# A two-layer decoder trunk on one core: memory values formed with tokens on the partitions, value halves side by side, and the step orders rewritten

## What is computed

```python
def memory_branch(q_mem, mem, norm_mem, w_mem_kv):
    k_m, v_m = jnp.split(rmsnorm(mem, norm_mem) @ w_mem_kv, 2, axis=-1)
    q, k, v = _heads(q_mem, 4), _heads(k_m, 4), _heads(v_m, 4)
    sc = jnp.einsum('bqhd,bkhd->bhqk', q, k) * 64 ** -0.5
    p = jax.nn.softmax(sc, axis=-1)
    return jnp.einsum('bhqk,bkhd->bqhd', p, v).reshape(q_mem.shape)
```

## Time and profile before

| what | us |
|---|---|
| median of 3 runs | 1217.27 (1217.08 to 1217.52) |
| the profiled execution | 1217.43 |
| its span, first to last instruction | 1215.6 |
| granted clock, mean | 0.999 of full speed |
| first memory tile begins | 14.9 |
| memory steps of layer A | 60 to 98 |
| attention of layer A and output projection | 98 to 285 |
| feed-forward part A | to 640 |
| memory steps of layer B | 655 to 694 |
| attention of layer B and output projection | 694 to 850 |

### The profile page before, as it was taken

The page is one execution under the profiler, slowest core; times in us unless marked ns, Lnnn a source line. Parts: engine busy times, 40 slices in busy tenths (PEclk is TensorE's granted clock), DMA queues, the critical chain, the costliest instruction groups (busy, mean ns, idle before and its releaser), DMA issues.

```text
span 1215.6 us, 16751 instructions
## 1 busy us (share of the span) xinstructions
PE 1189.6 (98%) x5963; PEld 986.1 (81%) x5963; DVE 799.4 (66%) x1197; ACT 553.7 (46%) x862; POOL 107.2 (9%) x94
## 2 busy tenths in 40 slices
...
GB/s 234 153 70 53 57 66 52 53 69 97 94 104 101 89 101 88 104 102 90 104 121 52 70 61 61 71 70 87 87 104 95 95 95 95 104 112 110 129 134 70
DMA packets 176386, 112.55 MB, mean 93 GB/s; under 512 B 20110, under 2 KB 168014, under 8 KB 176334
## 3 DMA queue, kind: packets, MB, share of 16 engines
...
q10 hardware_dynamic: 398, 0.16, 0.1%
...
## 4 chain that ended last, share of the span: by engine, by line
PE 92%; DVE 4%; ACT 2%; issue 1%; DMA 0%; ACTq 0%; POOL 0%; DVEq 0%; POOLq 0%
PE bank L1490 19%; PE bank L1491 19%; PE bank L1492 19%; PE bank L1830 4%; PE banks L1830 4%; PE bank L1801 4%; PE banks L1801 4%; PE banks L1719 1%; PE banks L1760 1%; PE bank L1693 1%; PE bank L1695 1%; PE bank L1694 1%; PE bank L1669 1%; PE bank L1671 1%; PE bank L1670 1%
## 5 line engine op out<-in xcount | busy, mean ns | idle before, releaser
L1490 PE MATMUL bank<-y_hi,w_hi 128*128 128x512 f32 x928 | 363.6, 392 | 0.0
L1491 PE MATMUL bank<-y_lo,w_hi 128*128 128x512 f32 x928 | 361.3, 389 | 0.0
L1492 PE MATMUL bank<-y_hi,w_lo 128*128 128x512 f32 x928 | 361.3, 389 | 0.0
L990 DVE TENSOR_TENSOR w_lo<-raw,w_hi 128x1024 fp32r<-128x1024 f32 x186 | 228.9, 1231 | 164.8 <-ACT w_hi L632 162.6
L632 ACT ACTIVATE w_hi<-raw 128x1024 fp32r<-128x1024 f32 x186 | 196.6, 1057 | 277.6 <-PE bank L1492 131.8
L1492 PEld LDWEIGHTS bank<-y_hi,w_lo 128*128 128x128 f32 x928 | 174.2, 188 | 36.5
L1490 PEld LDWEIGHTS bank<-y_hi,w_hi 128*128 128x128 f32 x928 | 174.3, 188 | 36.2
L1491 PEld LDWEIGHTS bank<-y_lo,w_hi 128*128 128x128 f32 x928 | 174.3, 188 | 34.7
L845 ACT ACTIVATE af<-af,conv 128x512 f32<-128x512 f32 x88 | 63.0, 716 | 34.5 <-DVE af L1244 34.5
L1244 DVE TENSOR_TENSOR af<-bank,rT 128x512 f32<-128x512 f32 x88 | 60.6, 688 | 25.8 <-PE bank L1492 25.7
L1251 DVE SCALAR_TENSOR_TENSOR af<-af,conv 128x510 f32<-128x510 f32 x88 | 66.1, 751 | 12.3 <-DVE af L1248 1.1
...
## 6 DMA issues: line engine op xcount, KB each, us to landing
...
```

The lines of the kernel that those rows point to most:

```text
L990: nc.vector.tensor_tensor(w_lo[:, m % SPLIT, :], raw[:, m % RAW, :], w_hi[:, m % SPLIT, :].bitcast(F32), ALU.subtract).then_inc(lo_done, 1)
L1490: mm(bank, w[0], y[0][:, k, :], start=(k == 0), stop=False)
L1491: mm(bank, w[0], y[1][:, k, :], start=False, stop=False)
L1492: last = mm(bank, w[1], y[0][:, k, :], start=False, stop=(k == KT - 1))
```

## The change

- Value tiles 2, 3, 6 and 7 of the memory projections are loaded as four k blocks of 256 output columns, and multiplied with the memory tokens as the stationary operand and the weights as the moving one. The result has tokens on the partitions. The two tiles of a layer add up in one bank, which holds 2 x 256 columns; `MEM_BANK` says which bank each of the eight tiles uses. The copies, transposes and gaps of zeros go. ACT and DVE split all four heads' values at once.
- `vm` holds the high and low half of a head's 64 columns side by side. A value product is 8 matmuls of 256 columns: 128-column weight by the high half, 64-column weight by the low half. The halves are added by two ACT copies and two DVE additions (entry D), POOL copies the sum to `oT_hi`, and DVE subtracts in an entry of its own, H. The next value product waits for the additions (`mo_add`).
- `squares_high(2)` and `squares_low(2)` are done after kv block 5, ahead of kv blocks 6 and 7 (`KV_SPLIT`).
- `sum_squares(0)` waits for `tab_ready` and no longer for the value splits. The first query tile waits for six evictions instead of seven.
- `SEQ_A` and `SEQ_B` are written anew.

```diff
@@ the memory values' layout
-        vm = [t[:, 1024:2560].rearrange("p (s k f x) -> p s k f x", s=2, k=2, f=2) for t in (am, bm)]
-        vm_gaps = [t[:, 1024:2560].rearrange("p (n x d) -> p n x d", n=8, x=3)[:, :, 1, :] for t in (am, bm)]
+        vm = [t[:, 1024:2048].rearrange("p (k f h s d) -> p k f h s d", k=2, f=2, h=2, s=2) for t in (am, bm)]
@@ the orders (layer A whole; layer B where the prediction speaks of it)
-        SEQ_A = [("F", 0, 3), ("C", 0), ("F", 3, 7), ("N", 0), ("F", 7, 11), ("B", 0), ("F", 11, 12), ("C", 1),
-                 ("F", 12, 15), ("N", 1), ("F", 15, 18), ("D", 0), ("F", 18, 19), ("B", 1), ("C", 2), ("F", 19, 23),
-                 ("N", 2), ("F", 23, 25), ("D", 1), ("F", 25, 26), ("B", 2), ("C", 3), ("N", 3), ("F", 26, 31),
-                 ("V", 0), ("F", 31, 32), ("D", 2), ("B", 3), ("F", 32, 37), ("D", 3)]
+        SEQ_A = [("F", 0, 1), ("C", 0), ("F", 1, 6), ("N", 0), ("F", 6, 9), ("C", 1), ("N", 1), ("B", 0),
+                 ("F", 9, 17), ("D", 0), ("B", 1), ("C", 2), ("F", 17, 21), ("H", 0), ("F", 21, 22), ("N", 2),
+                 ("F", 22, 23), ("D", 1), ("F", 23, 26), ("B", 2), ("C", 3), ("H", 1), ("F", 26, 28), ("N", 3),
+                 ("F", 28, 29), ("V", 0), ("F", 29, 31), ("D", 2), ("F", 31, 32), ("B", 3), ("F", 32, 35), ("H", 2),
+                 ("F", 35, 37), ("D", 3), ("H", 3)]
...
-                 ("P", 1, 0, 0, 1), ("D", 5), ("P", 1, 0, 1, 2), ("C", 7), ("B", 6), ("V", 0), ("N", 7),
-                 ("P", 1, 0, 2, 8), ("P", 1, 1, 0, 3), ("D", 6), ("B", 7), ("P", 1, 1, 3, 8), ("D", 7), ("S", 0),
+                 ("P", 1, 0, 0, 3), ("D", 5), ("B", 6), ("C", 7), ("H", 5), ("V", 0), ("N", 7), ("P", 1, 0, 3, 8),
+                 ("D", 6), ("P", 1, 1, 0, 3), ("B", 7), ("P", 1, 1, 3, 4), ("H", 6), ("P", 1, 1, 4, 8), ("D", 7),
...
-                 ("P", 2, 2, 0, 5), ("S", 2), ("P", 2, 2, 5, 8), ("P", 3, 0, 0, 6), ("V", 2), ("P", 3, 0, 6, 8),
-                 ("P", 3, 1, 0, 2), ("G", 0), ("P", 3, 1, 2, 8), ("P", 3, 2, 0, 1), ("R", 0), ("W", 0, 0),
-                 ("W", 0, 1), ("P", 3, 2, 1, 3), ("T", 0, 0), ("T", 0, 1), ("P", 3, 2, 3, 4), ("W", 0, 2),
+                 ("P", 2, 0, 3, 8), ("P", 2, 1, 0, 8), ("P", 2, 2, 0, 6), ("S", 2), ("P", 2, 2, 6, 8),
+                 ("P", 3, 0, 0, 6), ("V", 2), ("G", 0), ("P", 3, 0, 6, 8), ("P", 3, 1, 0, 8), ("R", 0),
+                 ("P", 3, 2, 0, 2), ("W", 0, 0), ("W", 0, 1), ("P", 3, 2, 2, 3), ("T", 0, 0), ("T", 0, 1),
...
-                 ("P", 4, 0, 0, 1), ("T", 0, 3), ("P", 4, 0, 1, 4), ("W", 0, 4), ("P", 4, 0, 4, 5), ("W", 0, 5),
-                 ("A", 0, 2), ("A", 0, 3), ("S", 3), ("P", 4, 0, 5, 8), ("P", 4, 1, 0, 2), ("T", 0, 4),
+                 ("P", 3, 2, 7, 8), ("P", 4, 0, 0, 1), ("T", 0, 2), ("T", 0, 3), ("P", 4, 0, 1, 4), ("S", 3),
+                 ("P", 4, 0, 4, 5), ("W", 0, 4), ("W", 0, 5), ("P", 4, 0, 5, 8), ("P", 4, 1, 0, 3), ("A", 0, 2),
+                 ("A", 0, 3), ("T", 0, 4), ("T", 0, 5), ("P", 4, 1, 3, 5), ("V", 3), ("P", 4, 1, 5, 6), ("W", 0, 6),
...
-                 ("A", 0, 7), ("S", 5), ("P", 4, 2, 4, 8), ("P", 5, 2, 0, 4), ("V", 4), ("P", 5, 2, 4, 7), ("G", 1),
-                 ("P", 5, 2, 7, 8), ("O", 0, 0), ("O", 0, 2), ("O", 0, 4), ("O", 0, 6), ("R", 1), ("O", 1, 0),
+                 ("P", 5, 2, 0, 6), ("V", 4), ("G", 1), ("P", 5, 2, 6, 8), ("O", 0, 0), ("O", 0, 2), ("O", 0, 4),
+                 ("O", 0, 6), ("R", 1), ("O", 1, 0), ("O", 1, 2), ("W", 1, 0), ("W", 1, 1), ("O", 1, 4), ("O", 1, 6),
...
+        MEM_BANK = (0, 1, 0, 0, 1, 0, 1, 1)
+        KV_SPLIT = 5
@@ gpsimd
-            for gap in vm_gaps:
-                nc.gpsimd.memset(gap.bitcast(F32), 0.0).then_inc(vm_zero, 1)
+            def mem_o_high(l):
+                for i in range(MH * l, MH * (l + 1)):
+                    f, hf = divmod(i % MH, 2)
+                    pool.wait_ge(mo_add, 2 * (i + 1))
+                    nc.gpsimd.tensor_scalar(oT_hi[:, 6 + f, half_queries(hf)], osum[:, 0:M], 1.0, 0.0,
+                                            ALU.mult, ALU.add).then_inc(mo_hi, 1)
...
@@ scalar
-                if n in (3, 4, 7):
-                    mem_v_high(mem_value(n - 1))
+                if f == 3:
+                    nc.scalar.activation(mem_v(l, 0), mem_v_sums(l), ACT.Copy).then_inc(v_hi, 2)
...
+            def mem_o_half(i):
                 act.wait_ge(mav, i + 1)
-                nc.scalar.activation(oT_hi[:, 6 + f, half_queries(hf)], OB[:, half_queries(hf)], ACT.Copy).then_inc(mo_hi, 1)
+                if i:
+                    act.wait_ge(mo_ev, i)
+                for hp in range(2):
+                    nc.scalar.activation(osum[DH * hp:DH * (hp + 1), 0:M], OB[DH:P, M * hp:M * (hp + 1)],
+                                         ACT.Copy).then_inc(mo_half, 1)
@@ vector
+            def mem_o_add(i):
+                for hp in range(2):
+                    dve.wait_ge(mo_half, 2 * i + hp + 1)
+                    a = slice(DH * hp, DH * (hp + 1))
+                    nc.vector.tensor_tensor(osum[a, 0:M], OB[0:DH, M * hp:M * (hp + 1)], osum[a, 0:M],
+                                            ALU.add).then_inc(mo_add, 1)
...
+                            if k == KV_SPLIT:
+                                squares_low(2)
@@ tensor
+            def mem_v_steps(n):
+                l, u = n // 4, n % 4 - 2
+                for kk in range(4):
+                    k = 4 * u + kk
+                    w = [t[:, n % SPLIT, M * kk:M * (kk + 1)] for t in (w_hi, w_lo)]
+                    for t in range(2):
+                        dst = banks[MEM_BANK[n]][:, M * t:M * (t + 1)]
+                        tok = slice(P * t, P * (t + 1))
+                        mm(dst, ym[:, l, 0, k, tok], w[0], start=(k == 0 and t == 0), stop=False, skip_group_check=True)
+                        mm(dst, ym[:, l, 0, k, tok], w[1], start=False, stop=False, skip_group_check=True)
+                        last = mm(dst, ym[:, l, 1, k, tok], w[0], start=False, stop=(k == KT - 1), skip_group_check=True)
+                last.then_inc(tile_done, 1)
...
-                if n >= 2:
-                    pe.wait_ge(evicted, n - 1)
+                if n in (2, 4, 5, 6):
+                    pe.wait_ge(evicted, {2: 1, 4: 2, 5: 4, 6: 5}[n])
...
                 if i:
-                    pe.wait_ge(mo_ev, i)
+                    pe.wait_ge(mo_add, 2 * i)
...
                     for hp in range(2):
-                        for s, (a, b) in enumerate(((0, 0), (0, 1), (1, 0))):
-                            last = mm(OB[:, half_queries(hf)], vm[l][:, a, kt, f, DH * hp:DH * hp + P],
+                        q = slice(M * hp, M * (hp + 1))
+                        mm(OB[:, q], vm[l][:, kt, f, hp].rearrange("p s d -> p (s d)"), pmTs[l][:, 0, kt, q],
+                           start=(kt == 0 and hp == 0), stop=False, skip_group_check=True)
+                        last = mm(OB[0:DH, q], vm[l][:, kt, f, hp, 0, :], pmTs[l][:, 1, kt, q], start=False, stop=(kt == 1),
+                                  skip_group_check=True)
```

More of the change, by code:

```diff
@@ L1481, in _, with steps @@
             mm = nc.tensor.matmul
-            def steps(n, m, ks, y, y_ready=None, width=T):
-                bank = banks[m % 2][:, 0:width]
+            def steps(n, m, ks, y, y_ready=None, width=T, bank=None):
+                bank = banks[m % 2 if bank is None else bank][:, 0:width]
                 for k in ks:
@@ L1536, in v_transpose @@
                 pe.wait_ge(vt_ready_of(iv)[0], vt_ready_of(iv)[1])
-                src = m_vT if count == 2 else vTs[iv >= 10]
-                dst = banks[(N_ATA + 3 * (iv - 4) + 2) % 2] if 4 <= iv < 10 else TR
-                if iv and dst is TR:
+                src = vTs[iv >= 10]
+                dst = banks[(N_ATA + 3 * (iv - 4) + 2) % 2] if iv < 10 else TR
+                if iv >= 10:
                     pe.wait_ge(v_lo, iv)
-                if iv == 0:
-                    pe.wait_ge(tab_ready, 1)
                 for t in range(count):
```

110 lines of the change are left out of this document (51 added, 59 removed), and 38 rows, old and new, of the table SEQ_B.

## The result

| | kernel before | changed kernel |
|---|---|---|
| median | 1217.27 us (1216.97 to 1218.04, 17 runs) | 1219.92 us (1218.47 to 1223.54, 17 runs) |
| ratio, 95% interval | | 1.0024 (1.0017 to 1.0031) |
| profiled execution, its span | 1217.43, 1215.6 | 1222.3, 1220.3 |
| mean granted clock of it | 0.999 | 0.993 |

Forecast were 1216.5 us and no change that can be told, with a range of 1212.0 to 1218.8. The result lies 3.4 us above the forecast, and its spread is new: the kernel before stays within 1.1 us, the changed one takes 5. The spread goes with the clock: at a mean granted clock of 0.997 the changed kernel took 1218.5 to 1218.9 us, at 0.993 1222.3 to 1223.5.

A forecast was written before the change was run, and what follows sets the result against it. TensorE, busy 98% of the span, was taken as the bound, so only its issue time and waits count. -2.2 - 3.4 - 1.4 + 1.8 + 2.3 + 3.8 - 1.7 = -0.8 gave 1216.5 us, range 1212.0 to 1218.8.

The forecast's parts named there:

- Part 6: Layer B, G directly behind V: TensorE waits 2.4 us at G 0 and 1.6 at G 1, net +3.8 us.
- Part 1: Memory projections at the start, values with tokens on the partitions: transposes go, tile 5 loses 0.7 us; net -2.2 us.
- Part 2: Memory heads' value product: 8 matmuls in 1.0 us instead of 12 in 1.43; over 8 steps -3.4 us.
- Part 3: Squares split between key/value blocks: the 1.3 us wait before the second sum of squares goes, -1.4 us with restart.
- Parts 4 and 5: New step orders of the memory heads: TensorE waits for DVE, +1.8 us in layer A and +2.3 us in layer B.
- rival (a): The orders hold: DVE keeps up and none of the memory heads' 4.1 us of waits appears; 1212.4 us, chance 0.27.
- Part 7: Rest of layer B's order: T 4 -1.2, A 4 -0.4, R 1 -0.6, S 3 +0.5; net -1.7 us.
- (b): H holds DVE: POOL's copy goes out late beside DVE's subtractions, six heads lose 0.6 us each; 1220.1 us, chance 0.10.
- (c): G directly behind V costs nothing, V's subtraction being done when G is reached; 1212.7 us, chance 0.05.

## Why the prediction was wrong, step by step

**Part 6 failed.** It forecast the two G waits to the point (2.12 and 1.56 us of idle time, with the restarts 2.3 and 1.7, where I had 2.4 and 1.6). But it priced them as time lost once, with nothing for the clock. They cost that and then a stretch at 1.2 GHz, some 4.8 us in the profiled execution and some 2.1 in the median of all runs. The earlier trace rows showed that TensorE would stand some 2 us; no row showed what such a stand does to the clock ahead of further work, since the longest wait of the kernel before after its first 15 us is 1.3 us. Its trace had a sign, though: the clock falls to 0.50 at 1212.8 us, 3.4 us after the last matmul, and that end alone makes the mean 0.999. The mean should have been read as something that the change could take away, with a bound of its own in the sum and the range. With 2.1 us more the forecast is 1218.6; the rest of the miss is below.

**Part 1** held: -2.3 against -2.2. Its tile 5 waits as forecast (0.54 us and its restart), but through the eviction count and not through the bank itself. The 0.2 us forecast before the sum of squares did not come; tile 3 waited 0.4 us for its weights' low half instead.

**Part 2** held: the value products take 0.93 to 1.02 us without a stop ahead and up to 1.18 behind one, against 1.0; over the eight it is 3.3 us less than before, 3.4 forecast. In the changed kernel, without a wait ahead:

```profile
78.76 0.28 PE L1658 MATMUL bank<-ar 128*128 128x256 f32 x1
78.88 0.28 PE L1660 MATMUL bank<-ar 128*64 128x256 f32 x1
78.99 0.28 PE L1658 MATMUL bank<-ar 128*128 128x256 f32 x1
```

So the lower bound, 0.12 a matmul as in the product of before, was right, and 0.16 and more comes only behind a stop (0.22 us behind the wait of D 0).

**Part 3** held: 1.3 us less with that edit alone in the kernel before, 1.4 forecast.

**Parts 4 and 5** held: with their restarts D 0 waits 0.95 us (0.9 forecast), D 3 0.4 (0.5), C 0 0.4 (0.15), B 3 0.3 (0.15), B 6 0.7 (0.75), B 7 0.95 (1.2). D 5 waited less than 0.2 instead of 0.3. Laying the queue of DVE out by hand from rows gave each wait to 0.3 us, and rival (a), which had 0.27 of the chance, fell. The runs with other orders add that these waits are DVE's load: they move more than they go.

**Part 7** was right on T 4 (gone) and R 1 (gone), and half right on S 3 (+0.3, +0.5 forecast). A 4 still waits 0.6 with its restart, where I took 0.4 off: worth 0.4 us. It missed the swap of S 1 and V 1, which stands in the order of the changed kernel though not in the lines of it printed ahead of the prediction: 0.7 us at 711 us, and 1.1 in the medians with and without. Those two, 1.1 us, are the larger part of the 1.3 that the clock leaves of the miss.

**Rivals.** (b) ended closest in time, 1220.1, by coincidence: its mechanism did not occur. (c) fell with the G waits.
